# A third operand buffer for the score levels of a chunked linear attention, with each level's exponents formed three masks ahead

## What is computed

```python
b = cumsum(log_g)                              # per key channel
attn[i, j] = sum_k q[i,k] * k[j,k] * exp(b[i,k] - b[j,k])     # j <= i
o = attn @ v + (q * exp(b)) @ S                # S: state of the chunks before
S = exp(b_last) * S + (k * exp(b_last - b)).T @ v
```

## Time and profile before

| | |
|---|---|
| median of 3 runs | 2333.84 us (2332.48 to 2334.25) |
| the profiled execution's own time | 2333.89 us |
| its span, first to last instruction | 2332.1 us |
| TensorE busy | 2251.2 us, 97% |
| VectorE busy | 1470.1 us, 63% |
| ScalarE busy | 1003.9 us, 43% |
| mean granted TensorE clock | 0.990 of full |

### The profile page before, as it was taken

How to read it: one execution, slowest core, us unless ns; L and a number is a source line. 1 busy time by engine, 2 the same in 40 slices (tenths; PEclk the granted TensorE clock), 3 DMA queues, 4 the chain that set the end, 5 groups by cost and what they waited for, 6 DMA issues and landing times.

```text
span 2332.1 us, 31489 instructions
## 1 busy us (share of the span) xinstructions
PE 2251.2 (97%) x10652; PEld 1866.0 (80%) x10652; DVE 1470.1 (63%) x2915; ACT 1003.9 (43%) x1738; POOL 0.2 (0%) x4
## 2 busy tenths in 40 slices
PE   6999999999999899999999999999999989999995
PEld 5888888888887688878878888888888867887884
DVE  5676677755556743466776777776555666336766
ACT  5444444433433622345545444544332454224442
POOL 0000000000000000000000000000000000000000
PEclk9999999999999999999999999999999999999997
DMA  4222222222222333354342222222222224342432
GB/s 171 81 81 90 72 79 83 90 73 91 73 89 82 127 122 117 102 196 130 108 145 73 90 83 79 72 90 88 76 85 77 89 72 156 117 124 99 125 121 99
DMA packets 72834, 234.15 MB, mean 100 GB/s; under 512 B 8352, under 2 KB 8608, under 8 KB 71872
## 3 DMA queue, kind: packets, MB, share of 16 engines
q1 hardware_dynamic: 72768, 233.28, 30.4%
HBM read 216.47 MB, written 16.78 MB: 100 GB/s over the span
## 4 chain that ended last, share of the span: by engine, by line
PE 82%; DVE 8%; ACT 4%; issue 2%; DMA 2%; DVEq 0%; SPq 0%; ACTq 0%
PE acc L407 24%; PE acc L408 24%; PE acc L409 24%; PE lv L479 3%; DVE w_lo L1074 2%; PE so L488 1%; PE so L490 1%; DMA w_raw<-in_slabs 1%; PE so L468 1%; DMA e_scratch<-work 1%; PE ms L457 1%; ACT w_hi L677 1%; DVE act_lo L1533 1%; ACT work L683 0%; DVE work L1250 0%
## 5 line engine op out<-in xcount | busy, mean ns | idle before, releaser
L407 PE MATMUL acc<-act_hi,w_lo 128*128 128x512 f32 x2880 | 1158.5, 402 | 16.0 <-ACT work L943 7.5
L408 PE MATMUL acc<-act_lo,w_hi 128*128 128x512 f32 x2880 | 1125.0, 391 | 0.0
L409 PE MATMUL acc<-act_hi,w_hi 128*128 128x512 f32 x2880 | 1124.7, 391 | 0.0
L407 PEld LDWEIGHTS acc<-act_hi,w_lo 128*128 128x128 f32 x2880 | 542.9, 189 | 135.1 <-issue 16.1
L409 PEld LDWEIGHTS acc<-act_hi,w_hi 128*128 128x128 f32 x2880 | 542.1, 188 | 114.7
L408 PEld LDWEIGHTS acc<-act_lo,w_hi 128*128 128x128 f32 x2880 | 543.3, 189 | 102.6 <-issue 1.2
L677 ACT CAST w_hi<-w_raw 128x1024 fp32r<-128x1024 f32 x360 | 361.6, 1047 | 530.2 <-PE acc L409 503.3
L1074 DVE TENSOR_TENSOR w_lo<-w_raw,w_hi 128x1024 fp32r<-128x1024 f32 x360 | 424.4, 1219 | 48.6 <-ACT w_hi L677 48.6
L722 ACT ACTIVATE work<-work 128x512 f32<-128x512 f32 x168 | 106.0, 631 | 292.4 <-DVE work L1101 292.4
L1107 DVE TENSOR_TENSOR work<-work 128x256 f32<-128x256 f32 x168 | 71.5, 426 | 133.8 <-ACT work L722 133.6
L479 PEld LDWEIGHTS lv<-work 128*128 128x128 f32 x672 | 99.5, 190 | 26.0 <-DVE work L1108 13.9
(11 more groups left out here) (169 smaller groups left out, 1573.8 us busy)
## 6 DMA issues: line engine op xcount, KB each, us to landing
w_raw<-in_slabs SPq DMA_DIRECT2D x360, 512.0 KB, 4.1
e_scratch<-work SPq DMA_DIRECT2D x32, 256.0 KB, 2.1
work<-in_x_feat SPq DMA_DIRECT2D x32, 256.0 KB, 2.6
work<-e_scratch SPq DMA_DIRECT2D x32, 256.0 KB, 2.6
out<-feat SPq DMA_DIRECT2D x32, 256.0 KB, 2.3
work<-in_x SPq DMA_DIRECT2D x7, 1024.0 KB, 4.9
work<-in_x SPq DMA_DIRECT2D x2, 512.0 KB, 10.4
work<-in_p SPq DMA_DIRECT2D x2, 512.0 KB, 3.6
```

The source lines that it names most:

```text
L407: nc.tensor.matmul(ps, lhs_lo, rhs_hi, start=start, stop=False)
L408: nc.tensor.matmul(ps, lhs_hi, rhs_lo, start=False, stop=False)
L409: return nc.tensor.matmul(ps, lhs_hi, rhs_hi, start=False, stop=stop)
```

## The change

A third buffer `x_lv2` of 128 x 512 float32 is added, and level l uses `x_lv[l % 3]` on all three engines. The PSUM banks of the levels stay two. `rec_first` ends with the arguments of level 2; `next_level(R, l)` is now mask of level l, products of level l + 2, arguments of level l + 3 (none past level 6). In the last head the arguments of level 2 stand ahead of `next_level(r0, 0)`, and the arguments of level 6 move from E tile 0 to `next_level(R, 3)`. ScalarE's and TensorE's orders stay, and no instruction is added or removed but for the buffer's address.

```diff
-        x_lv = [unit(19), unit(20)]
+        x_lv = [unit(19), unit(20), sb("x_lv2", [P, TH])[:, :]]
...
 level (TensorE), rec_level (ScalarE), level_arg, level_mul (VectorE):
-                x_lv[l % 2]
+                x_lv[l % 3]
...
                 level_arg(R, 1)
                 level_mul(R, 1)
+                level_arg(R, 2)
 
             def next_level(R, l):
                 mask_level(R, l)
-                level_arg(R, l + 2)
                 level_mul(R, l + 2)
+                if l + 3 < LEVELS:
+                    level_arg(R, l + 3)
...
                 if last:
                     level_arg(r0, 1)
                     level_mul(r0, 1)
+                    level_arg(r0, 2)
                     next_level(r0, 0)
...
                     if e == 0:
                         mask_level(R, 4)
-                        level_arg(R, 6)
                     if e == 1:
                         level_mul(R, 6)
```

More of the change, by code:

```diff
@@ L476, in level @@
                 for c in range(2):
-                    queries = x_lv[l % 2][:, 2 * C:4 * C].rearrange("p (b n) -> p b n", b=2)
+                    queries = x_lv[l % 3][:, 2 * C:4 * C].rearrange("p (b n) -> p b n", b=2)
                     scores = lv_ps[l % 2][:, 0:2 * C].rearrange("p (b n) -> p b n", b=2)
-                    last = nc.tensor.matmul(scores[:, :, c * half:(c + 1) * half], x_lv[l % 2][:, c * C:(c + 1) * C],
+                    last = nc.tensor.matmul(scores[:, :, c * half:(c + 1) * half], x_lv[l % 3][:, c * C:(c + 1) * C],
                                             queries[:, :, c * half:(c + 1) * half], start=True, stop=True)
@@ L721, in rec_level @@
                 act.wait_ge(lv_arg, R * LEVELS + (l + 1))
-                A(x_lv[l % 2], x_lv[l % 2], ACT.Exp).then_inc(lv_exp, 1)
+                A(x_lv[l % 3], x_lv[l % 3], ACT.Exp).then_inc(lv_exp, 1)
             def k_copy(R):
@@ L1098, in level_arg @@
                 s = 1 << l
-                x, mid = x_lv[l % 2], last_lower(b_t, s)
+                x, mid = x_lv[l % 3], last_lower(b_t, s)
                 st.mark(v.tensor_tensor(level_keys(x, s), mid, lower_tokens(b_t, s), ALU.subtract))
@@ L1105, in level_mul @@
                 s = 1 << l
-                keys, queries = level_keys(x_lv[l % 2], s), level_queries(x_lv[l % 2], s)
+                keys, queries = level_keys(x_lv[l % 3], s), level_queries(x_lv[l % 3], s)
                 st.mark(v.tensor_tensor(keys, keys, lower_tokens(k_t, s), ALU.mult))
```

## The result

The changed kernel takes 2316.54 us (median of 4 runs, 2314.60 to 2317.29) against 2334.05 of the kernel before: a ratio of 0.9925, 95% interval 0.9907 to 0.9942. The profiled execution took 2317.29 us, its span 2315.5: 16.6 us less than before. The forecast was 2321.5, so it is faster, and the gain was under-forecast by 4 to 5 us. The kernel before, run again beside the experiments, had medians of 2332.8 to 2333.5, so some 16.5 us is the better figure for the gain. One run of the kernel before, beside the last experiment, took 3257.44 us at a clock of 0.655 and is left out of these medians.

What follows compares the result with a forecast made beforehand. TensorE, busy throughout 24 to 740 us, bounds the kernel, so only its waits in each half's last head can pay: 2 x 6.2 = 12.4 us off 2333.89 gives 2321.5 us, range 2316.5 to 2328.5.

Steps and rivals of the forecast that it cites:

- Steps 1 to 4: Last head, up to level 4: arguments made ahead; products 4 end 4.45 us earlier, TensorE's wait falls from 3.34 to 0.45.
- Step 7: E tiles 0 to 2: Exp 6 loses its 1.38 us wait for arguments; tile 2's square comes 6.2 us earlier.
- Step 8: From E tile 2's square to the readout: everything moves by 6.2 us unchanged, later waits included; store landings could shift 2.4.
- the one at 2137: Half clock lasting 6.82 us in the second half; its going away was priced at 3.4 us, outside the main forecast.
- the ring: E stage's stores, slab loads and copies, possibly setting its pace; if stores meet loads worse, 3.3 us per half is left.
- The E stage gives half of it back: Rival: E stage's stores meet slab loads worse, leaving 3.3 us gain per half, 2327.3 us; chance 0.18.
- The wait only changes its name: Rival: level 4 waits as long for low parts, casts or `p`; 2332.3 us, chance 0.09.
- The clock falls elsewhere: Rival: eight waits of 1.3 to 1.8 us could bring half clock, 1.7 or 3.4 each; up to 2341.9 us, chance 0.04.
- More: Rival: the clock fall at 2137 goes (3.4 us) or the first E stores land in 2.1 us; 2317, chance 0.07.
- the slower rival: Rival: clock falls behind eight remaining waits of 1.3 to 1.8 us make it slower, up to 2341.9 us; chance 0.04.

Runs made afterwards that it cites:

- the last experiment: Kernel before the change, with the slab load behind the store of E tile 5 and mask 6 at tile 3: 2327.33 us, ratio 0.9976.
- level 6 late: Changed kernel with the arguments of level 6 back at E tile 0: 2319.13 us.
- last head alone: New order in the last head of each half only, old order in the middle heads: 2316.66 us, ratio 0.9935.
- buffer alone: Kernel before with the third buffer added and its old order kept: 2333.36 us, ratio 1.0004.
- middle heads alone: New order in the 22 middle heads only, old order in the last head of each half: 2330.96 us, ratio 0.9992.
- before with two edits: Kernel before the change, slab load moved behind the store of E tile 5 and mask 6 moved to tile 3: 2327.33 us, ratio 0.9976.
- `p` first: Changed kernel with the casts and low parts of p ahead of four y_high and two y_low: 2316.70 us.
- the stores and mask 6: Changed kernel with the slab load behind the store of E tile 5 and mask 6 at tile 3: 2310.09 us, ratio to before 0.9907.

## Why the prediction was right or wrong

**Where the gain lies: right.** Nothing that can be told came from the middle heads, and the last heads alone give all of it, shown by the two halves of the change run apart. The buffer's place is worth nothing, shown too. That VectorE's idle time before products can fall by 69 us and buy no microsecond while TensorE never waits is the plainest lesson of the case. The prediction had 96 us: it left out that level 5 of the GLA iterations keeps a wait of up to 2.8 us.

**Steps 1 to 4: right in place and size.** Low weights end at 752.04 (751.95 forecast), `k_copy` starts at 751.02 (751.1), `log_sigmoid` at 754.01 (754.05), level 4 at 759.88 (759.9), with a wait of 0.52 (0.45) and the clock at full. The 3.34 us wait was replaced by what was late next, the low parts of `p`: 1.10 us where I had 1.5, TensorE being ready at 762.0 (761.8) and they at 763.0 (763.2). Level 5 comes 5.13 earlier (5.1), the square of tile 2 6.45 (6.2).

**Step 7: right sum, wrong reason.** I put 1.38 us of it down to level 6's arguments being made three masks ahead. With them back at E tile 0 the Exp waits 0.14 us. The wait was long before the change because VectorE came to tile 0 late, behind the arguments, the Exp and the products of level 5; with those out of the way it is gone by itself. Before, VectorE added tile 0's square at 771.64, 1.0 us after ScalarE had finished it; with level 6 late it adds it at 765.40, 0.1 us after.

**Step 8: the term that was mis-sized, put at nothing.** I carried every later wait over unchanged, the half clock behind the readout and the one at 2137 among them. Compared matmul by matmul, the profiled pair differs by 6.5 us at the row sums of the first half, still by 6.5 at the start of the second half's last head, by 13.9 at its row sums, and by 16.6 at the end. So the two stretches gave 6.5 and 7.3 (6.2 each forecast), and 2.7 came after them, in the G stage of the second half, where the wait at 2123.5 is 2.44 us for 2.95 (0.5) and no half clock stands behind it (2.2). In the first half the readout at full clock ran 1.1 us ahead, and the ring took it back, with a 2.20 us wait before tile 11 where there had been 1.29; in the second half it was kept. Taking it back was largely chance: it hangs on the store of tile 7 that landed after 4.4 us, and where the same order met a landing of 2.4 (last head alone) the row sums came 1.8 us earlier. Together that is 0.3 + 1.1 + 2.7 = 4.1 of the 4.2 us between the forecast of 12.4 and the 16.6 of the pair.

The 2.7 us of the G stage are not shown to be the change's. Of the four profiles in which the last head keeps its old order (before, buffer alone, middle heads alone, before with two edits) only the first has a fall there, and against the profile with the buffer alone the changed kernel's span is just 12.4 us shorter. The medians differ by more, 16.3 to 17.5 us; 13.9 of it lies in the two stretches, and where the rest comes from is open. That the result fell inside the range, 0.04 us from its end, is luck.

**The rivals.** "The E stage gives half of it back": it doesn't; what it does is absorb small leads (0.8 with `p` first) that come without the stores and mask 6. "The wait only changes its name": 1.1 of 3.3 us did. "The clock falls elsewhere": no wait of the changed kernel was followed by a fall before its last 25 us, though five were between 2.02 and 2.44 us. "More", put at 2317 and given 0.07, is what came. But its total is near by luck: it priced the one fall at 2137 at 3.4 us, which was worth 2.2, and the rest came from the readouts' falls and a shorter wait. Five falls stood in the profile of before ahead of its last 25 us. Two stood behind the level 4 waits of 3.34 and 3.70, which the forecast removed; three, behind waits of 1.97, 2.05 and 2.95 us, were free to go or stay, and I allowed for one. The slower rival counted seven waits without a fall; the profile before has nine from 1.29 to 1.77 us.

**What I would do otherwise.** The clock behind a wait that is not removed is a thing to be priced on both sides, like an unknown cost. I had the rows on both sides of it (1.77 without, 1.97 with a fall) and used them for the slower rival, and for one fall in "more".

## What to carry to other kernels

A lead of one step in a software pipeline pays only where the consumer of its result is waiting: look at the ends of the loop, where the cover runs out, before counting idle time in its middle. Where two gates stand on one path (here a DMA queue's order and a mask), removing one gives the other its wait; test them together before either is called worthless. And when a stretch has waits that end in a slower clock, compare variants by distances inside the stretch, summed over its repeats, and not by medians alone, which hold the falls elsewhere.

## What the runs showed that I had not expected

The same wait at the same place is or is not followed by half clock. In the run with `p` first the readouts wait 2.79 and 2.78 us, and the clock behind them is 1.00 and 0.50:

```profile
778.00:781.40 3.40, 3.40 (x16) 2.73 (x15) 0.51 (x2) 0.84 (x2) 0.00 (x0) 1.00 0.58 211
1912.77:1916.18 3.41, 3.41 (x9) 2.67 (x9) 0.71 (x2) 1.33 (x3) 0.00 (x0) 0.50 0.43 163
```

Over the profiled runs, waits from 1.91 us on were seen with a fall behind them, and waits of up to 2.93 us without one; of the 98 waits between 1.0 and 1.88 us in the 14 profiles none had one, so the slower rival, which rested on waits of 1.3 to 1.8 us, had been given its chance on something that these runs never show. This is at least a part of how runs of one kernel come to differ by up to 7 us here: 10 runs of the kernel with the buffer alone lie between 2329.6 us, at a clock of 0.992, and 2337.0, at 0.990. The Trainium skill ("TensorE: Matmul & The Clock Gate", Part 1) says that the slow matmuls of one kernel vary between runs because the hardware's watch doesn't follow the kernel; the runs here agree, and two equal waits in one execution differ as well.
